# Two-layer diffusion backbone on one core: modulation vectors as weights-stationary products, two in the opening and four inside the first projection; split value products in the neighbourhood attention

## The reference

```python
mod_l = (silu(c) @ ada_w[layer] + ada_b[layer])[:, None, :]
mod_c = (silu(c_ctx) @ ada_w[layer] + ada_b[layer])[None, None, :]
sh1, sc1, g1, sh2, sc2, g2 = split(mod_l, 6)
h_l = rmsnorm(x, norm1_g[layer]) * (1 + sc1) + sh1
o_l, o_c = mixer(h_l @ w_in, h_c @ w_in, ...)      # even: differential || windowed; odd: latent || neighbourhood
x = x + g1 * (o_l @ w_out[layer])
x = x + g2 * sq_relu_mlp(modulate(x, norm2_g[layer], sh2, sc2), mlp_w1[layer], mlp_w2[layer])
```

## Time and profile before

| | |
|---|---|
| three runs, median (lowest to highest) | 3914.27 us (3912.47 to 3916.89) |
| the profiled execution, its own time | 3915.37 us |
| its span in the profile | 3913.6 us |
| PE busy in the span | 3586.3 us, 92% |
| DVE, ACT, POOL busy | 2010.5, 1298.2, 176.4 us |
| opening | from 0 to about 114 us |
| first projection `pb` | about 119 to 298 us |
| neighbourhood attention `ad` | about 2795 to 3062 us |

### The profile page before, as it was taken

How to read it: one execution, slowest core, us unless ns; L and a number is a source line. 1 busy time by engine, 2 the same in 40 slices (tenths; PEclk the granted TensorE clock), 3 DMA queues, 4 the chain that set the end, 5 groups by cost and what they waited for, 6 DMA issues and landing times. The chain is left out here.

```text
span 3913.6 us, 47915 instructions
## 1 busy us (share of the span) xinstructions
PE 3586.3 (92%) x17932; PEld 2876.5 (73%) x17932; DVE 2010.5 (51%) x2906; ACT 1298.2 (33%) x2312; POOL 176.4 (5%) x186
## 2 busy tenths in 40 slices
PE   8798798897899999999988979799799889999999
PEld 2586565786788888888877768577577688888887
DVE  2456564786663444443445455588544373333333
ACT  2453243564431111111125445466333351111111
POOL 0210010000120000000001000000000020000000
PEclk9898799898999999999998989799899999999999
DMA  8335554422322222221214344333344331111112
GB/s 313 132 129 188 144 134 89 115 75 86 88 82 58 68 62 70 60 60 55 68 51 154 139 148 139 96 73 73 81 102 92 108 97 46 46 48 48 54 52 66
DMA packets 439684, 370.72 MB, mean 95 GB/s; under 512 B 103509, under 2 KB 382437, under 8 KB 434405
## 3 DMA queue, kind: packets, MB, share of 16 engines
q1 hardware_dynamic: 439525, 368.61, 33.0%
HBM read 280.86 MB, written 87.69 MB: 94 GB/s over the span
## 5 line engine op out<-in xcount | busy, mean ns | idle before, releaser
L2033 DVE SCALAR_TENSOR_TENSOR xT<-ps,mods,xT 128x1024 f32<-128x1024 f32 x192 | 189.4, 1014 | 424.2 <-PE ps L2247 424.2
L2247 PE MATMUL ps<-e_gh,e_w2h 128*128 128x512 f32 x1280 | 356.2, 376 | 5.9 <-DVE e_w2l L2489 3.6
L2247 PE MATMUL ps<-e_gl,e_w2h 128*128 128x512 f32 x1280 | 352.2, 373 | 0.0
L2247 PE MATMUL ps<-e_gh,e_w2l 128*128 128x512 f32 x1280 | 351.9, 373 | 0.0
L2539 DVE TENSOR_TENSOR e_plain<-e_plain 128x1280 f32<-128x1280 f32 (+1 forms) x64 | 87.0, 1359 | 479.6 <-ACT e_plain L2404 479.6
L2247 PE MATMUL ps<-e_hl,e_w1h 128*128 128x512 f32 (+1 forms) x1200 | 327.2, 370 | 0.0
L2247 PE MATMUL ps<-e_hh,e_w1h 128*128 128x512 f32 (+1 forms) x1200 | 327.2, 370 | 0.0
L2247 PE MATMUL ps<-e_hh,e_w1l 128*128 128x512 f32 (+1 forms) x1200 | 327.1, 370 | 0.0
L2404 ACT ACTIVATE e_plain<-ps 128x1280 f32<-128x1280 f32 (+1 forms) x64 | 72.7, 1135 | 756.6 <-PE ps L2247 755.1
L2247 PEld LDWEIGHTS ps<-e_gh,e_w2h 128*128 128x128 f32 x1280 | 224.5, 190 | 55.4 <-DVE e_gl L2543 8.0
L2247 PEld LDWEIGHTS ps<-e_gh,e_w2l 128*128 128x128 f32 x1280 | 225.9, 190 | 43.4
(11 more groups left out here) (349 smaller groups left out, 7502.9 us busy)
## 6 DMA issues: line engine op xcount, KB each, us to landing
e_raw<-in_mlp_w SPq DMA_DIRECT2D x64, 512.0 KB, 4.2
e_raw<-in_mlp_w SPq DMA_DIRECT2D x128, 256.0 KB, 3.0
aw<-in_ada_w SPq DMA_DIRECT2D x12, 2048.0 KB, 9.2
e_raw<-in_w_out SPq DMA_DIRECT2D x48, 512.0 KB, 4.0
rstd<-in_ada_w SPq DMA_DIRECT2D x64, 384.0 KB, 3.3
qkC<-pc_stage SPq DMA_DIRECT2D x72, 192.0 KB, 2.7
hT<-pb_hb SPq DMA_DIRECT2D x10, 1024.0 KB, 5.4
pa_hb<-hT SPq DMA_DIRECT2D x10, 1024.0 KB, 5.1
```

The source lines that it names most:

```text
L2033: ins = k.nc.vector.scalar_tensor_tensor(out=x, in0=ps, scalar=k.mods[:, layer, gate, bass.ds(n, 1), w], in1=x, op0=ALU.mult, op1=ALU.add)
L2247: mm = pe.matmul(k.ps[:, SB * (e % 2) + b, 0:n], w[:, e % 2, f], m[:, f, c0:c0 + n], start=(f == 0 and x == 0), stop=(f == nf - 1 and x == 2))
```

## The change

Three edits.

- **Modulation vectors in the opening.** `ada_w` is now the weight: a "vector" n is 128 columns of it (512 KB, runs of 512 bytes in memory), 8 products of a 128x128 weight with 2 streamed columns, which leave the result already turned in PSUM. The copy to rows, the turning and their buffers are gone. The opening computes only the first two modulation vectors of 1024 (16 of the 48 pieces), with 8 buffers. The sums of squares are now taken chunk by chunk (three chunks of tokens, two products each) between the steps.
- **The other four inside `pb`.** 32 pieces, four in each of the token tiles 1 to 8, two after the first job and one after each of the others. They use the `wraw` buffers, once the weights are cut, in three pairs, and PSUM bank 3, so the jobs rotate over three banks instead of four. The loads stand in SP's list behind the stores of each job. The same DVE instructions that add the bias are called here by `modulation_vector`.
- **`attend` takes `split` apart from `parts`.** `ad` keeps its way of computing scores but gets the split value product of `ac`. `ab` stays as it was.

```diff
-        for n in range(N_HALVES):
-            steps += [("ada", n)] + [("x", t) for t in (XB + 2 * n, XB + 2 * n + 1) if t < NT]
+        for n in range(NV):
+            steps += [("ada", n)] + ([("x", XB + n)] if XB + n < NT else [])
...
-                    for f in range(KT):
-                        mm = pe.matmul(k.ps[0:2, AB + n % 2, :], sil2[:, f], aw[:, n % WB, f], start=(f == 0), stop=(f == KT - 1))
+                    for f in range(KT):
+                        mm = pe.matmul(k.ps[:, AB + n // KT, col:col + 2], aw[:, n % WB, f], sil2[:, f], start=(f == 0), stop=(f == KT - 1))
...
-                        mm = pe.matmul(k.ps[:, TB + c, 0:n], k.ones[:], acc[:, c0:c0 + n], start=True, stop=True)
+                    for a in range(2):
+                        mm = pe.matmul(k.ps[:, SUMB, 0:n], k.ones[:], both(c)[:, a], start=(a == 0), stop=(a == 1))
...
+    MB, AB = (4, None) if vectors is None else (3, 3)
...
+        first = (t - 1) * per_tile
+        return [(first, first + 1), (first + 2,), (first + 3,)][j]
...
+                def fetch_vector(n):
+                    if n >= NV:
+                        return
+                    if n < 3:
+                        sp.wait_ge(s.wlo, len(slices) - RAW + 2 * n + 2)
+                    else:
+                        sp.wait_ge(s.av, n - 2)
+                    sp.dma_start(v_tile(n), v_dram[FIRST_VECTORS * KT + n]).then_inc(v_sem(n), 16)
...
+                def vector(n):
+                    pe.wait_ge(v_sem(n), v_loaded(n))
+                    if n >= KT and n % KT == 0:
+                        pe.wait_ge(s.modd, n // KT)
+                    col = 2 * (n % KT)
+                    for f in range(KT):
+                        mm = pe.matmul(k.ps[:, AB, col:col + 2], v_tile(n)[:, f], k.sil2[:, f], start=(f == 0), stop=(f == KT - 1))
+                    mm.then_inc(s.av, 1)
...
-    split = parts == "three"
+    three = parts == "three"
...
-               "two", HD, k.mix[1], 512, bias=bias_loader(k))
+               "two", True, HD, k.mix[1], 512, bias=bias_loader(k))
```

More of the change, by code:

```diff
@@ L277, in _ @@
                     else:
[L278 to L283, removed]
+                        vector(n)
+                    for c in sums_at(y):
+                        sums(c)
             @block.scalar
@@ L288, in _, with squares, roots @@
                 nc.scalar.activation(tmp[:], cols[:, 0:16], ACT.Exp, scale=-1.0).then_inc(s.neg, 1)
[L290 to L310, removed]
+                def squares(c, g):
+                    c0, n = chunks[c]
+                    act.wait_ge(s.xcpA, (c0 + n) // P)
+                    act.wait_ge(s.xcpD, (c0 + n) // P)
+                    x, here = k.xT[:, 2 * g:2 * g + 2, c0:c0 + n], c * (PAIRS - 1) + g - 1
+                    if g and here >= 2:
+                        act.wait_ge(s.acc, here - 1)
+                    nc.scalar.activation(both(c) if g == 0 else sq[:, here % 2, :, 0:n], x, ACT.Square).then_inc(s.sq, 1)
+                def roots(c):
+                    c0, n = chunks[c]
+                    act.wait_ge(s.sum, c + 1)
+                    nc.scalar.activation(k.rstd[:, c0:c0 + n], k.ps[:, SUMB, 0:n], ACT.Sqrt, bias=k.eps[:],
+                                         scale=1.0 / D_MODEL).then_inc(s.root, 1)
+                for y, (what, n) in enumerate(steps):
                     if what == "x":
@@ L314, in _ @@
                                        k.ps[:, TB + 2 * (n % 2), :].rearrange("p (f q) -> p f q", q=P)).then_inc(s.xcpA, 1)
[L315 to L321, removed]
+                    for c, g in pairs_at(y):
+                        squares(c, g)
+                    for c in roots_at(y):
+                        roots(c)
             @block.vector
@@ L374, in _, with accumulate, inverses @@
-                for what, n in steps:
+                def accumulate(c, g):
+                    n, here = chunks[c][1], c * (PAIRS - 1) + g - 1
+                    dve.wait_ge(s.sq, c * PAIRS + g + 1)
+                    if g > 1:
+                        dve.wait_ge(s.acc, here)
+                    nc.vector.tensor_tensor(both(c), both(c), sq[:, here % 2, :, 0:n], ALU.add).then_inc(s.acc, 1)
+                def inverses(c):
+                    c0, n = chunks[c]
+                    dve.wait_ge(s.root, c + 1)
+                    nc.vector.reciprocal(k.rstd[:, c0:c0 + n], k.rstd[:, c0:c0 + n])
@@ L375, in _, with modulation @@
+                def modulation(j):
+                    dve.wait_ge(s.av, (j + 1) * KT)
+                    modulation_vector(k, dve, j, k.ps[:, AB + j, 0:2 * KT], s.modd, j + 1, s.m0)
+                for y, (what, n) in enumerate(steps):
                     if what == "x":
@@ L498, in _ @@
                         fetch_h(1)
+                for n in range(3):
+                    fetch_vector(n)
                 for n, (t, j) in enumerate(jobs):
@@ L1279, in steps_of_head, with attend @@
     return out, blocks
-def attend(k, name, pieces, heads, load_head, parts, v_width, mix, mix_col, sink=None, bias=None, beside=None):
+def attend(k, name, pieces, heads, load_head, parts, split, v_width, mix, mix_col, sink=None, bias=None, beside=None):
     nc = k.nc
@@ L1346, in sb @@
             return st.enter_context(nc.sbuf_tensor(f"{name}_{nm}", shape, dt))
-        D = MLA_QK if split else HD
-        if split:
+        D = MLA_QK if three else HD
+        if three:
             q_sb, k_sb = sb("q", [D + 1, 2, 2, TOK], F32R), sb("k", [D + 1, 2, 2, TOK], F32R)
@@ L1504, in score @@
                     out = scores(x)[:, 0:t.n * P]
[L1506 to L1507 removed]
+                    prods = ((1, 0), (0, 1)) if three else ((0, 0),)
+                    r = D if three else 2 * D
                     if x % NS == 0:
```

158 lines of the change are left out of this document (83 added, 75 removed).

## The result

The changed kernel takes 3932.55 us (median of 7 runs, 3923.76 to 3935.54); the kernel before, beside it, 3914.27 us (7 runs, 3908.31 to 3917.03). The ratio is 1.0039, with a 95% interval of 1.0028 to 1.005: slower by some 15 us (11 to 20) by the ratio, and the two medians are 18.3 us apart. I had forecast 3947 us, 32 us more. The direction is right, the size is about twice too large.

The account below looks back on a forecast made before the run. PE was taken as the bound in all three touched stretches. Opening -34, pieces +55.4, clock +20 and `ad` -9 made +32 us on 3915.4, so 3947 us after 1.1 us median correction; own range 3930 to 3968, whole 3908 to 3980.

Parts of the forecast that it names:

- The opening: Stretch before `pb`: ends at 80 us against 114, a gain of 34 us, mostly at low clock.
- The six pairs: Opening: six pairs of piece and token tile, 6 x 5.1 = 30.6 us at low clock.
- the ten pieces: Opening: ten pieces in a row after the sums of squares, 34 us at low clock.
- `pb`, +75.4 forecast: First projection: 55.4 us added for 32 pieces, plus 20 us for falls of the clock.
- Twelve falls: `pb`: eight falls behind double pieces, the rest behind turned heads and a piece; 1.65 us each, 20 us.
- The loads, the three banks, SP's and DVE's order at nothing: `pb`: load traffic, three banks instead of four, delayed stores and DVE's wait are covered and cost nothing.
- `ad`, -9 forecast: Neighbourhood attention: split value products save PE 19 us, half given back for DVE's 80 us of new work; -9 us.
- waiting for L1728: Expected sign in `ad`: PE waits for DVE's row maximum while the stage is some 9 us shorter.
- The rival in which DVE becomes the bound: `ad`: DVE's list falls behind and PE waits; +8 instead of -9 us, 3965 us; chance 0.15.
- Nothing elsewhere: Stages outside the opening, `pb` and `ad`: the forecast sum has no term for them.
- the clock holds: Rival, opening and `pb`: full clock throughout; -63 + 55.4 + 0 - 19 = -27, 3888 us; chance 0.10.
- the clock holds in part: Rival: opening ends at 68 us, six falls in `pb`, `ad` -12; +7, 3922 us; chance 0.13.

Follow-up runs that it names:

- pb_eighth: Changed kernel with one product of eight in each of the 32 pieces of `pb`, loads, bank and waits kept: 3858.94 us, ratio 0.9851 to the kernel before.
- vectors: Changed kernel with `ad` not split, so only the modulation vectors are moved: 3946.48 us, ratio 1.0093 to the kernel before.
- before_2: The kernel before, unchanged, profiled again; its two repeat profiles had single runs of 3911.53 and 3910.47 us.
- after_2: The changed kernel, unchanged, profiled again; its two repeat profiles had single runs of 3926.15 and 3932.47 us.
- the streamed one: Changed kernel with the opening's two vectors computed in the old streamed form, four halves with 2 KB runs: 3919.18 us, ratio 1.0017 to the kernel before.
- the filled opening: Changed kernel with an unread 384-column fp32r product added behind every second product of the opening's pieces: 3930.32 us, ratio 1.0035 to the kernel before.

## Why the prediction was right in direction and wrong in size

- **The opening, -34 forecast, -38.2 measured.** Right in mechanism: 0.213 us a record in the burst, and a clock that comes back for a while. In the first profile the last piece ended at 74.2 us and not 80. The six pairs took 20.8 us (13.05 to 23.37 and 26.92 to 37.39) where I had 30.6 at low clock, less 4 us for the whole opening; the ten pieces 31 instead of 34; the sums 8.9 instead of 6.5, since they ran at 0.50 themselves, and the clock rose only behind the first two of the three. It is also the least certain part: in nine profiles of kernels that share this opening unchanged the first product of `pb` starts between 82.5 and 89.0 us, so 4 us are within what one profile varies.
- **`pb`, +75.4 forecast, +77.2 measured.** Right, and both of its terms by experiment: 55.4 for the pieces (spread at full clock they lengthen a tile from 14.95 to 22.2 us, 58 in all; with one product in eight it is 15.84) and 20 for the clock (spreading gave back 22 us by the runs, 18 by the profile). Twelve falls were forecast; the tiles' excess (turned heads start at 118.59 and, eight tiles on, at 311.98 us: 193.4, less 8 x 14.95 and 55.4) is 18.4 or eleven falls. Which bursts cause most of them was right too: parting the double piece gave 1.0004, where 1.0005 was expected.
- **The loads, the three banks, SP's and DVE's order at nothing.** Right to 2 us, by `pb_eighth`.
- **`ad`, -9 forecast, -15.4 measured. This step failed.** I had 19 us less of PE and wrote "So I give back half". The sum of DVE's new work, 80 us, was right (81 us by its groups), but not that it reaches PE: PE's wait for the maxima is 4.5 us before and after, where the prediction had it waiting for L1728. The argument was a busy share of 190 in 215 us (175 measured) and an in-order list. DVE idled 115.0 us before its maxima: the 81 us fit in that. A second subtraction at every second step, 38 us more over `ad`, costs at most 7 us there, and one at every step, 75 us more, 29. So the term should have been the whole saving of PE: 19 by my count, and 17 in the profiles of the split alone (204.7 and 204.0 us beside 221.6). The rival in which DVE becomes the bound falls with it.
- **Nothing elsewhere, by leaving it out of the sum. This failed too, and its cause is open.** The other half of the miss lies there: `pc` is 5.5 us shorter, and the rest of the untouched part 2.5 (3.1 less 0.6), which is within the spread. `pc` takes 239.7 to 241.1 us in the three profiles of the kernel before, 239.1 and 236.3 with the split alone, and 231.2 to 234.9 in all thirteen profiles of kernels with the new `project`, `vectors` among them. So most of it goes with the moved vectors and not with the split. PE waits less in `pc` for the cut weights and for staging:

```profile
PE ps L897 <- DVE pc_wl L1055: 18.1, 5, 12.4
PE ps L936 <- ACT pc_stage L1024: 14.4, 11, 4.2
```

before (`before_2`), and in the changed kernel (`after_2`)

```profile
PE ps L951 <- DVE pc_wl L1109: 15.2, 5, 12.5
PE ps L990 <- ACT pc_stage L1078: 13.4, 13, 4.3
```

No instruction of `pc` differs. What the change does to it stays open.

The sum of the misses, in the means of three profiles: 4.2 us in the opening, 6.4 in `ad` and 8.0 in parts not touched, less 1.8 in `pb`, are the 16.8 us between 32.4 and 15.6. The rival "the clock holds" (3888 us) was wrong in both places where it could have held. The result lies inside the forecast's own range, near its low end, and between the forecast and the rival "the clock holds in part" (3922 us), whose -12 for `ad` was nearer and whose opening and `pb` were not.

## What to carry to other kernels

Here a product with a fresh 128x128 weight and two columns took 0.22 us (two records of 0.108) at full clock, and in long rows, where the granted clock fell to 0.50, twice that. Put behind wide products one by one, the same work in `pb` cost 59 us instead of 77 (242.0 and 260.2 less 182.9).

Moving work from one PE-bound stage to another gains only where PE waits. The four vectors cost 55.4 us in `pb`, without the clock, and had cost 58 in the opening (eight halves at 7.3). PE does wait in this part of the kernel, as much now as before: from the opening's end to the first product of `pa` in the changed kernel

```profile
PE ps L574 <- DVE pb_wl L701: 22.0, 5, 9.4
PE ps L574 <- DVE pa_wl L701: 12.8, 1, 12.8
```

and 21.2 and 13.1 us in the kernel before. The pieces stand in none of these waits; no run tried to put them there. In the first tile of `pb` the buffers that they use still hold its weights.

Before you charge an engine's new work to the path, look at what the bound engine waits for it, and at how long it idles ahead of the instruction that others wait for.

## What the runs showed of the hardware

- The loads of `ada_w` in runs of 512 bytes move 282 GB/s with the DMA engines full, beside 387 for the same matrix in runs of 2 KB, with token tiles among them. The changed opening from 35 to 43 us, where nothing but pieces of `ada_w` is loaded, and the streamed one from 15 to 40 us:

```profile
DMA packets 4481, 2.26 MB, mean 282 GB/s; under 512 B 71, under 2 KB 4481, under 8 KB 4481
```

```profile
DMA packets 4110, 9.67 MB, mean 387 GB/s; under 512 B 158, under 2 KB 158, under 8 KB 4109
```

  That is the 282 that I had taken from stores. The Trainium skill ("DMA: Bandwidth & Descriptors", Specifications) gives 512 bytes as the least size for full rate; here that size is about a quarter short of it.
- Transposes count for the clock: the filled opening holds 1.00 with token tiles among the pieces and falls once they are gone, and the first 32 transposes of the kernel, with no other product among them, get faster on their way. The Trainium skill ("TensorE: Matmul & The Clock Gate", Part 4: PE-mode transpose) says that they do not count as PE-busy the same way and that full clock does not engage for them; the measurement decides against the latter. They do not always suffice: in the changed opening token tiles and pieces alternate at 1.00 from 28 to 34 us, behind sums of squares, but the clock falls at about 34.4 us in the middle of that alternation, and from 15 to 27 us it is 0.60 in the mean.
- The same opening differs by 6.5 us between nine profiles (first product of `pb` at 82.5 to 89.0 us; 83.6, 85.5 and 88.3 in the three of the changed kernel), mostly for the clock: from 15 to 75 us the granted clock is 0.62 in the quickest and 0.55 in the slowest.
